# A prologue with X and scale rows loaded by turns and four un-normalised chunks

## The reference, cut to what matters

```python
def short_conv_layer(x, c, mod_w, mod_b, norm_g, w_in, conv_w, w_out):
    shift, scale, gate = modulation(c, mod_w, mod_b, 3)
    h = modulated_norm(x, norm_g, shift, scale)
    proj = h @ w_in
    b_gate, c_gate, u, z = jnp.split(proj, 4, axis=-1)
    y = b_gate * causal_dwconv(c_gate * u, conv_w)
    y = y * jax.nn.silu(z)
    return x + gate[:, None, :] * (y @ w_out)
```

## Time and profile before

| what | value |
|---|---|
| median of three runs | 2802.17 us (2800.43 to 2805.7) |
| profiled execution: span | 2802.3 us (its time is not listed beside the span) |
| TensorE busy | 2707.3 us, 97% |
| VectorE, ScalarE, GpSimd busy | 1614.1, 1189.8, 1109.0 us |
| first wide matmul; chunk 4 begins; chunk 7 begins | 29.80; 88.28; 123.33 us |
| fill of the normalised operand ends | 81.26 us |

### The profile page before, as it was taken

One profiled execution on the slowest core, in us unless ns is written; L12 is line 12 of the kernel. 1 busy time (PEld: TensorE's weight loads), 2 busy tenths in 40 slices (PEclk: granted clock), 3 DMA queues, 4 the chain that ended last, 5 costly groups with the idle time before them and its releaser, 6 DMA issues.

```text
span 2802.3 us, 38646 instructions
## 1 busy us (share of the span) xinstructions
PE 2707.3 (97%) x13208; PEld 2150.3 (77%) x13208; DVE 1614.1 (58%) x2120; ACT 1189.8 (42%) x1779; POOL 1109.0 (40%) x753
## 2 busy tenths in 40 slices
PE   6999999999999998999999999999999999989998
PEld 4788888787777776878886777777788888868886
DVE  7744443304676776583015555554436766788888
ACT  4211123323555555442236667765434433334442
POOL 1222222121555554212221111211123988858886
PEclk9999999999999999999999999999999999999999
DMA  5333321344211213113330101101443343374442
GB/s 228 128 127 120 120 98 45 103 146 140 76 54 45 82 52 114 59 38 111 121 108 31 38 32 37 38 30 61 150 158 120 128 161 141 136 259 158 159 161 92
DMA packets 102110, 294.74 MB, mean 105 GB/s; under 512 B 9856, under 2 KB 10496, under 8 KB 101504
## 3 DMA queue, kind: packets, MB, share of 16 engines
q1 hardware_dynamic: 102016, 293.56, 29.7%
HBM read 220.12 MB, written 73.40 MB: 105 GB/s over the span
## 4 chain that ended last, share of the span: by engine, by line
PE 60%; issue 25%; POOL 6%; DVE 4%; ACT 3%; DMA 1%; POOLq 0%; SPq 0%; ACTq 0%; DVEq 0%
PE PS L847 27%; PE PS L1331 10%; PE PS L1383 5%; PE PS L1077 5%; POOL WL L2747 3%; PE PS L1049 2%; PE PS L982 2%; PE PS L1011 2%; PE PS L1026 2%; PE PS L1235 2%; POOL dL L2860 1%; PE PS L1216 1%; DVE dM L2679 1%; DVE bC L2296 1%; PE PS L1175 1%
## 5 line engine op out<-in xcount | busy, mean ns | idle before, releaser
L2747 POOL TENSOR_TENSOR WL<-WR,WH 128x1024 fp32r<-128x1024 f32 x147 | 367.7, 2501 | 1359.9 <-ACT WH L1421 1252.6
L847 PE MATMUL PS<-HH,WH 128*128 128x512 f32 x1712 | 546.0, 400 | 19.4 <-POOL WL L2747 5.9
L847 PE MATMUL PS<-HL,WH 128*128 128x512 f32 x1712 | 531.6, 392 | 0.0
L847 PE MATMUL PS<-HH,WL 128*128 128x512 f32 x1712 | 530.0, 391 | 0.0
L847 PEld LDWEIGHTS PS<-HH,WH 128*128 128x128 f32 x1712 | 315.4, 189 | 95.9 <-issue 26.3
L847 PEld LDWEIGHTS PS<-HL,WH 128*128 128x128 f32 x1712 | 323.4, 189 | 69.3
L847 PEld LDWEIGHTS PS<-HH,WL 128*128 128x128 f32 x1712 | 323.2, 189 | 69.3
L1421 ACT ACTIVATE WH<-WR 128x1024 fp32r<-128x1024 f32 x147 | 155.6, 1059 | 324.1 <-PE PS L847 226.6
L2771 POOL TENSOR_TENSOR bB<-bB,bC 128x256 f32<-128x256 f32 (+7 forms) x128 | 191.2, 1504 | 191.1 <-DVE bC L2296 191.1
L2296 DVE TENSOR_TENSOR_SCAN bC<-bN,EPSC 128x256 f32<-128x256 f32 (+7 forms) x128 | 222.7, 1751 | 57.3 <-ACT bN L1607 52.4
L2679 DVE TENSOR_TENSOR dM<-PS,dM 128x512 f32<-128x512 f32 x212 | 136.2, 678 | 1.6 <-PE PS L1383 1.2
(11 more groups left out here) (348 smaller groups left out, 5618.7 us busy)
## 6 DMA issues: line engine op xcount, KB each, us to landing
WR<-wst SPq DMA_DIRECT2D x149, 512.0 KB, 3.4
uRAW<-wst SPq DMA_DIRECT2D x32, 512.0 KB, 4.8
hid<-uT SPq DMA_DIRECT2D x32, 512.0 KB, 2.8
dRAW<-wst SPq DMA_DIRECT2D x64, 256.0 KB, 3.6
HLF<-hid SPq DMA_DIRECT2D x28, 512.0 KB, 8.9
GLF<-hid SPq DMA_DIRECT2D x28, 512.0 KB, 8.1
TMP<-mods SPq DMA_DIRECT2D x24, 512.0 KB, 4.2
MR<-mods SPq DMA_DIRECT2D x24, 512.0 KB, 5.3
```

Source lines behind the costliest of these rows:

```text
L847: last = pe.matmul(PS[:, dst0 + q:dst0 + q + HALF], l, rr[:, k * S + q:k * S + q + HALF], start=a, stop=z)
L2747: pool.tensor_tensor(WL[slot][:, :], WR0[:, :], WH[slot][:, :].bitcast(F32), ALU.subtract).then_inc(w_lo, 1)
```

## The change

Loads come in the order X tile, scale row, X tile, scale row, with the first weights between them; the eight shift rows come last, into the buffers of the scale rows. VectorE's first pass is then only the scale products, coefficients and low parts. The squares go to four buffers of their own, and **GpSimd** adds them one by one into `XSUM`; TensorE sums it once. **Four** chunks, 0 to 3, run on the un-normalised tiles: 0 and 1 step by step with the tiles, 2 and 3 behind them, with weights in their own buffers `WHX`, `WLX` and in PSUM pairs 2 and 3. The shift columns of all four chunks are made at one place, inside chunk 3 behind its second step (`shift_columns`): 64 fp32r matmuls of two columns, a high and a low part of the shift. VectorE makes shift rows 0 to 3; for rows 4 to 7 GpSimd multiplies and ScalarE sums. The fill follows chunk 3, and chunks 4 and 5 are the interleaved ones that follow the fill. Chunk 3's output is read out by VectorE in the fill, ahead of its seventh tile (`early_out(3, 3)`), and frees pair 1 for chunk 5. The other small preparations (`GQ8`, `GFE`) stand behind the fill.

Core of the diff:

```diff
+            for k in range(KT):
+                sp.dma_start(kt(X, k), xt[:, k * S:(k + 1) * S]).then_inc(ld_k[k], 16)
+                sp.dma_start(kt(MRAW, k), mods[KT + k]).then_inc(ld_k[k], 16)
+                if k == 0:
+                    sp.dma_start(WR0[:, :], wst[0]).then_inc(ld_w, 16)
...
+            for k in range(KT):
+                sp.wait_ge(mod_done, k + 1)
+                sp.wait_ge(ld_k[k], 32)
+                sp.dma_start(kt(MRAW, k), mods[k]).then_inc(ld_k[k], 16)
...
             sp.wait_ge(f_lo, FILL["a"] + KT)
+            sp.wait_ge(free[1], USED["ain"][1] + 2)
...
+            def shift_columns():
+
+                pe.wait_ge(a_rows, 2)
+                pe.wait_ge(free[1], u[1] + 1)
+                for m, (hi, lo) in enumerate(((WH[0], WL[0]), (WH[1], WL[1]), (WHX[0], WLX[0]), (WHX[1], WLX[1]))):
+                    for k in range(KT):
+                        for half in (hi, lo):
+                            last = pe.matmul(PS[:, S + 2 * m:S + 2 * m + 2], half[:, k * P:(k + 1) * P],
+                                             SHR[:, 2 * k:2 * k + 2], start=k == 0 and half is hi,
+                                             stop=k == KT - 1 and half is lo)
+                last.then_inc(a_cols, 1)
...
+            for k in range(KT):
+                if k == KT - 1:
+                    sum_squares(SQ["aout"], XSUM, dst=3 * S)
+                pe.wait_ge(a_raw_lo, k + 1)
+                step(C_AIN, 0, 0, HH, HL, k)
+                step(C_AIN + 1, 1, 1, HH, HL, k)
+            for k in range(KT):
+                early_step(0, k, None)
+            pe.wait_ge(rs, 1)
+            for k in range(KT):
+                early_step(1, k, a_raw_read)
+                if k == 1:
+                    shift_columns()
...
+            for k in range(KT // 2, KT):
+                act.wait_ge(a_mul, k - KT // 2 + 1)
+                act.activation(kt(MRAW, k), kt(MRAW, k), ACT.Identity, accum_out=col(MOD, k)).then_inc(mod_done, 1)
...
                 if k == 2:
-                    split_w(2, 0)
...
+                    split_w(4, 0)
+                    act.activation(SM[:, 12:16], PS[:, S + 1:S + 8:2], ACT.Identity).then_inc(a_shift, 1)
+                if k == 4:
+                    split_w(5, 1)
+                    act.wait_ge(a_shift, 2)
+                    act.activation(AE[1][:, :], AE[1][:, :], ACT.Identity, bias=SM[:, 9:10]).then_inc(ain_cu, 1)
...
+            for n in range(KT - 1):
+                pool.wait_ge(sq, n + 1)
+                if n:
+                    pool.wait_ge(sq_added, n)
+                first = XSQ[0] if n == 0 else XSUM
+                pool.tensor_tensor(XSUM[:, :], first[:, :], XSQ[(n + 1) % 4][:, :], ALU.add).then_inc(sq_added, 1)
+            for m, raw in enumerate((WR0, WR3)):
+                pool.wait_ge(w_hi, 3 + m)
+                pool.tensor_tensor(WLX[m][:, :], raw[:, :], WHX[m][:, :].bitcast(F32), ALU.subtract).then_inc(w_lo, 1)
+            pool.wait_ge(s_sc, 1)
+            for k in range(KT // 2, KT):
+                pool.wait_ge(ld_k[k], 48)
+                pool.tensor_tensor(kt(MRAW, k), kt(MRAW, k), CB, ALU.mult).then_inc(a_mul, 1)
```

More of the change, by code:

```diff
@@ L416, in block_kernel @@
         ld_cb = sem("ld_cb")
-        ld_x = [sem(f"ld_x{i}") for i in range(4)]
+        ld_vec = sem("ld_vec")
+        ld_w3 = sem("ld_w3")
         ld_k = [sem(f"ld_k{i}") for i in range(KT)]
@@ L903, in _, with early_step @@
             pe.wait_ge(s_const, 1)
[L905 to L910, removed]
-            u = USED["ain"]
+            u = USED["ain"]
+            def early_step(m, k, last_sem):
+                pair = 2 + m
+                b = slice(k * P, (k + 1) * P)
+                if k == 0:
+                    pe.wait_ge(w_hi, C_AIN + 3 + m)
+                    pe.wait_ge(w_lo, C_AIN + 3 + m)
+                last = mm3(pair * S, WHX[m][:, b], WLX[m][:, b], HH, HL, k, k == 0, k == KT - 1)
+                if k == KT - 1:
+                    last.then_inc(chunk_done, 1)
+                elif last_sem is not None:
+                    last.then_inc(last_sem, 1)
@@ L914, in input_chunks @@
             def input_chunks(j, first=False):
                 if first:
[L916 to L927, removed]
@@ L934, in _ @@
+            with pe.Fori(2, KT) as j:
                 input_chunks(j)
@@ L2153, in raw_low @@
                                          op0=ALU.mult, op1=ALU.subtract).then_inc(a_raw_lo, 1)
[L2155 to L2158 removed]
+            scale(0)
+            raw_low(0)
+            scale(1)
+            for k in range(2, KT):
+                scale(k)
                 raw_low(k - 1)
             raw_low(KT - 1)
[L2162 to L2166 removed]
@@ L2168, in _ @@
-            fill_lo("a", 1, lambda k: col(COEF, k), 0, before=first_input)
+            for k in range(KT // 2):
+                dve.wait_ge(ld_k[k], 48)
+                modulation(col(MOD, k), kt(MRAW, k))
+            dve.wait_ge(mod_done, 2 * KT)
+            links(dve.tensor_tensor(MOD[:, 0:KT], MOD[:, 0:KT], VEC[:, _V["mod_b"]:_V["mod_b"] + KT], ALU.add))
+            dve.tensor_copy(SHR[:, 0:2 * KT:2], MOD[:, 0:KT]).then_inc(a_rows, 1)
+            dve.wait_ge(a_rows, 1)
+            dve.tensor_tensor(SHR[:, 1:2 * KT:2], MOD[:, 0:KT], SHR[:, 0:2 * KT:2].bitcast(F32), ALU.subtract).then_inc(a_rows, 1)
@@ new lines, in early_out @@
+            def early_out(m, pair):
+                dve.wait_ge(chunk_done, C_AIN + m + 2)
+                dve.tensor_tensor(AE[m][:, :], PAIR[pair], T[0], ALU.mult).then_inc(free[m % 2], 1)
+            dve.wait_ge(rs, 1)
+            early_out(0, 0)
+            early_out(1, 1)
+            def first_input(k):
+                if k == 1:
+                    early_out(2, 2)
+                if k == 4:
+                    dve.wait_ge(a_shift, 1)
+                    dve.tensor_tensor(SM[:, 8:12], PS[:, S:S + 8:2], SM[:, 12:16], ALU.add).then_inc(a_shift, 1)
+                if k == 6:
+                    dve.wait_ge(w_lo, 4)
+                    early_out(3, 3)
@@ L2196, in input_products @@
                     modulations(j, 2, 2)
-                dve.wait_ge(chunk_done, 4 * j + 4)
-                dve.tensor_tensor(T[3], PAIR[0], T[3], ALU.mult).then_inc(free[0], 1)
-                if not first:
+                if first:
+                    dve.scalar_tensor_tensor(out=T[3], in0=AE[2][:, :], scalar=SM[:, 10:11], in1=T[3],
+                                             op0=ALU.add, op1=ALU.mult).then_inc(a_shift, 1)
+                else:
+                    dve.wait_ge(chunk_done, 4 * j + 4)
+                    dve.tensor_tensor(T[3], PAIR[0], T[3], ALU.mult).then_inc(free[0], 1)
                     modulations(j, 4, 2)
```

168 lines of the change are left out of this document (81 added, 87 removed).

## The result

| | us |
|---|---|
| before, median of 4 runs | 2801.3 (2799.6 to 2805.7) |
| changed, median of 4 runs | 2832.5 (2829.9 to 2833.7) |
| ratio, 95% interval | 1.0108 [1.0094, 1.0123] |

The changed kernel is slower by 31 us. The forecast was 2821, with a range that ended at 2829. Its profiled execution has a span of 2830.9 us, 28.6 over that of the earlier trace rows.

The account below looks back on a forecast made before the run. The prediction took chunk 7's start on TensorE, at 123.33 us and hanging on VectorE's product, as the bound. Prologue terms put it at 142.3, 19 us later: 2802.3 + 19 = 2821, range 2805 to 2829.

Parts of the forecast that it names:

- Step 2: Prologue: GpSimd's and VectorE's alternating operations, 35.1 and 23.1 us, added to a start at 9.9, end at 68.1.
- step 4: TensorE's un-normalised steps: last tile ready at 49.4; TensorE stands at 66.8 and waits 5.8 us for the shift columns.
- the signs: What would show the forecast right: low parts about 3.5 us each, GpSimd hardly pausing from 10 to 68, columns near 73.
- Step 3: Last shift row's sum on ScalarE, VectorE's small work and two PSUM outputs: the shift columns may start at 72.6.
- Step 5: The 64 shift-column matmuls inside chunk 3: at half clock 13.6 us, to 86.2; at full clock 7.0.
- The rival with the full clock: Shift columns at the full clock, or cheaper: 6.6 us less there, 1.2 in the step after; 2813 us, chance 0.19.
- the one in which gain and loss cancel: Cheap columns and modulation loads already landed: chunk 7 starts within 5.6 us of 123.33; 2797 to 2808, chance 0.08.
- Step 6: Filling the normalised operand after chunk 3 on ScalarE, GpSimd and VectorE: ends at 108.2, where before it ended at 81.26.
- Step 7: VectorE's gate products, eight modulation rows and PSUM product after the fill: chunk 7 starts at 142.3, 19 us later.
- The rule on bursts: Un-normalised steps: bursts shorter than their data wait restart at half rate; columns would start near 75.5, sum 2824.
- The rival that more is late: Chunks 8 and 9 wait too, or the clock stays low longer after the 8 us wait: over 2829, chance 0.05.
- The rival that the loads set the pace: Prologue tiles come every 2.5 us with the loads, engine turns not biting: 2789 to 2796 us, chance 0.10.

## Why the prediction was wrong

- **The step that failed** is the sentence behind the sum: "Behind it TensorE runs without a gap in this stretch, and the change touches nothing there; a shift at chunk 7 is a shift of the end." The change touched the addresses of `GH` and `GL`. By the medians that cost 12.5 us (2832.5 against 2820.0; by the ratios to the kernel before 11.8), and 11.0 in the kernel before (2813.2 against 2802.2). With the addresses put back the schedule takes 2820.0, 1 us from the forecast. A part of this nearness is luck: in that kernel chunk 7 came 16.5 us late and not 19, and some 1 us more was lost between it and 415 us.
- Step 1 had the first split at 9.9; it came at 10.76.
- Step 2, the sum of turns, had the last shift product end at 68.1; it ended at 66.6. So the sum held to 1.5 us, and so did the 49.4 of step 4 for the last un-normalised tile (48.6). From start to end it was 55.8 us for 58.2. But "the turns are never free" was not so: GpSimd idled 11.3 us in that stretch, waiting for ScalarE, and the sum held since VectorE's operations ran in these gaps.
- Of the signs, the low parts came out against the forecast: six of the eight took 1.27 us and not 3.5, as they ran in GpSimd's gaps; what sat out the additions were the coefficients, 2.2 us each.
- Step 3 had the columns at 72.6; they came at 70.81. TensorE stood at 66.9 (66.8 forecast) and waited 3.9 instead of 5.8.
- Step 5 had 13.6 us for the columns at the half clock; it was 12.4. The first twelve still ran at 0.11 us, the other 52 at 0.213. The rival with the full clock fell, and with it the one in which gain and loss cancel, which needed cheap columns.
- Step 6 had the fill's end at 108.2; it was 105.7 (104.41 + 1.28).
- Step 7 had chunk 7 at 142.3; it came at 139.30, and the wait of 8 us was 7.5. The sum was 3 us too large, and had been so from the end of the columns on (83.2 for 86.2). The eight rows and the product took 22.2 us (117.03 to 139.25), within the forecast's 21.5 to 23.2; in 7.3 of them VectorE waited for the rows' loads.
- The rule on bursts: TensorE did fall to the half clock behind the wait of 3.74 us at 28.94, and that tile's two steps took over 5 us (28.94 to 34.2). But no wait stands ahead of the next tile, then 0.83 us and then 1.60, so the waits took up what the slow burst lost, and the columns did not start at 75.5. By the forecast's own numbers a tile of 4.8 us with 2.7 of steps leaves a wait of 2.1, so these bursts were not shorter than the wait, and the rule as the prediction puts it was not one for them. The sum without it was nearer.
- The rival that more is late gave a time over 2829 and that is what came, but not by its mechanism: no chunk behind the seventh waits up to 330 us. The rival that the loads set the pace fell: the low parts came every 4.6 us and not every 2.5.

## What to carry to other kernels

A new tile, however small, moves all that the allocator places behind it; before a stage is called untouched, compare the addresses of the operands that TensorE streams there, and put small tiles where they push nothing. Where VectorE and GpSimd take turns at SBUF, work handed from one to the other counts at its full length on the receiver: add up both engines' operations as one queue, and then see what each of them waits for, since here a ring through ScalarE came to nearly the same sum. A run of narrow matmuls can cost the clock although TensorE never idles in it; with wide ones between, it didn't.

## What the runs showed of the hardware

A 128 x 512 fp32r matmul took 389 ns with its moving operand (the 128 x 512 part of `GH` or `GL` that a product reads beside its weights) where the kernel before had it, 395 with it 128 bytes further and 389 again at 256. The 2208 products of `GH` and `GL` paid for it with 11 us in all, and no wait shows it. And with the rows on VectorE some 43 back-to-back matmuls of two columns, with no idle time ahead, ran at 0.11 us each until the granted clock fell to the lower level near 71 us (35 of them, until near 70, with SHR moved as well). In groups of sixteen with six wide ones between, all 64 ran at 0.11. Why was not taken further.
